# Two transformer blocks on one core: pooling output by token kind, latent-KV columns for context first

## What is computed

```
# pooling layer, for latent tokens and for context tokens
y   = (pooled * silu(gate)) @ w_out            # 2048 x 2048
x   = x   + gate_l * rms_norm(y_lat, post_norm)
ctx = ctx + gate_c * rms_norm(y_ctx, post_norm)
# attention layer
h_lat = rms_norm(x, pre_norm)   * (1 + scale_l) + shift_l
h_ctx = rms_norm(ctx, pre_norm) * (1 + scale_c) + shift_c
proj  = h @ w_in      # 512 cq | 512 ckv | 64 kr | 2048 gate
```

## Time and profile before

| | us |
|---|---|
| median of three runs | 2441.93 (2441.76 to 2445.03) |
| the profiled execution | 2442.31 |
| its span | 2440.5 |
| PE busy in the span | 2247.1 (92%) |
| DVE, ACT busy | 1453.0 (60%), 929.4 (38%) |

### The profile page before, as it was taken

The page is one execution under the profiler, slowest core; times in us unless marked ns, Lnnn a source line. Parts: engine busy times, 40 slices in busy tenths (PEclk is TensorE's granted clock), DMA queues, the critical chain, the costliest instruction groups (busy, mean ns, idle before and its releaser), DMA issues.

```text
span 2440.5 us, 32191 instructions
## 1 busy us (share of the span) xinstructions
PE 2247.1 (92%) x13350; PEld 1819.7 (75%) x13350; DVE 1453.0 (60%) x1894; ACT 929.4 (38%) x1258; POOL 212.1 (9%) x400
## 2 busy tenths in 40 slices
PE   5989899999889999989999999999957999999896
PEld 2678778877878878867777888877836889677575
DVE  1345678777636777746867575676747573334253
ACT  2225445544426545546422222233222333334242
POOL 2211110110010110010000010000010010000000
PEclk8989999999999999999999999999978999999898
DMA  9987576777687676675665464555525585211152
GB/s 373 400 251 275 199 258 216 270 267 258 213 272 264 233 264 230 213 287 188 229 199 181 147 216 139 189 163 178 187 87 176 167 279 148 59 54 56 34 207 103
DMA packets 214858, 496.15 MB, mean 203 GB/s; under 512 B 31616, under 2 KB 35840, under 8 KB 212672
## 3 DMA queue, kind: packets, MB, share of 16 engines
q1 hardware_dynamic: 157728, 278.47, 34.0%
q0 software_dynamic: 56848, 215.38, 25.7%
q10 hardware_dynamic: 144, 0.36, 0.0%
HBM read 485.75 MB, written 8.39 MB: 202 GB/s over the span
## 4 chain that ended last, share of the span: by engine, by line
PE 75%; DVE 9%; DMA 9%; ACT 4%; issue 2%; SPq 1%; POOL 0%; DVEq 0%; ACTq 0%; POOLq 0%
PE ps L733 21%; PE ps L734 20%; PE ps L735 20%; DMA w_raw<-in_w_in 3%; PE ps L788 2%; DMA ada_raw<-in_ada_w 2%; PE ps L1287 1%; PE ps L1285 1%; PE ps L1304 1%; DVE ada_acc L1907 1%; DVE wl L1994 1%; DMA w_raw<-in_w_out 1%; ACT wh L1392 1%; DMA ub<-in_ctx 1%; DMA rsw<-in_ada_w 1%
## 5 line engine op out<-in xcount | busy, mean ns | idle before, releaser
L1994 DVE TENSOR_TENSOR wl<-w_raw,wh 128x1024 fp32r<-128x1024 f32 x280 | 334.8, 1221 | 268.3 <-ACT wh L1392 267.6
L1392 ACT ACTIVATE wh<-w_raw 128x1024 fp32r<-128x1024 f32 x280 | 291.6, 1056 | 439.2 <-PE ps L735 263.9
L733 PE MATMUL ps<-hh,wh 128*128 128x256 f32 x1280 | 375.3, 293 | 11.9 <-DVE hl L2045 7.7
L1987 DVE TENSOR_TENSOR wl<-w_raw,wh 128x1024 fp32r<-128x1024 f32 x194 | 235.1, 1221 | 231.6 <-ACT wh L1445 188.9
L734 PE MATMUL ps<-hh,wl 128*128 128x256 f32 x1280 | 364.0, 284 | 0.0
L735 PE MATMUL ps<-hl,wh 128*128 128x256 f32 x1280 | 363.4, 284 | 0.0
L1907 DVE SCALAR_TENSOR_TENSOR ada_acc<-ada_raw,cpad,ada_acc 128x1024 f32<-128x1024 f32 x272 | 340.7, 1280 | 21.2 <-DMA ada_raw<-in_ada_w 19.0
L1445 ACT ACTIVATE wh<-w_raw 128x1024 fp32r<-128x1024 f32 x162 | 170.1, 1058 | 445.9 <-PE ps L735 407.7
L733 PEld LDWEIGHTS ps<-hh,wh 128*128 128x128 f32 x1280 | 246.0, 192 | 36.2 <-issue 19.7
L733 PE MATMUL ps<-wh,act_hl 128*128 128x512 f32 x640 | 254.9, 398 | 6.7 <-DVE wl L1987 6.7
L734 PE MATMUL ps<-wh,act_hl 128*128 128x512 f32 x640 | 254.3, 397 | 0.0
(11 more groups left out here) (355 smaller groups left out, 3434.7 us busy)
## 6 DMA issues: line engine op xcount, KB each, us to landing
ada_raw<-in_ada_w POOLq DMA_DIRECT2D x272, 512.0 KB, 5.0
w_raw<-in_w_in SPq DMA_DIRECT2D x208, 512.0 KB, 6.5
w_raw<-in_pool_in SPq DMA_DIRECT2D x72, 512.0 KB, 4.6
w_raw<-in_w_out SPq DMA_DIRECT2D x64, 512.0 KB, 5.7
ada_fourth<-in_ada_w POOLq DMA_DIRECT2D x48, 512.0 KB, 6.2
w_raw<-in_mla_in SPq DMA_DIRECT2D x48, 512.0 KB, 4.7
w_raw<-in_pool_out SPq DMA_DIRECT2D x32, 512.0 KB, 4.5
w_raw<-in_mla_out SPq DMA_DIRECT2D x32, 512.0 KB, 3.8
```

The lines of the kernel that those rows point to most:

```text
L733: pe.matmul(dst, ah, bh, start=start, stop=False, skip_group_check=True)
L1392: act.activation(wh[:, g % RING, :], w_raw[:, g % RING, :], ACT.Copy).then_inc(w_hi, 1)
L1987: dve.tensor_tensor(wl[:, r, :], w_raw[:, r, :], wh[:, r, :].bitcast(F32), ALU.subtract).then_inc(w_lo, 1)
L1994: dve.tensor_tensor(wl[:, g % RING, :], w_raw[:, g % RING, :], wh[:, g % RING, :].bitcast(F32), ALU.subtract).then_inc(w_lo, 1)
```

## The change

It cuts the last two quarters of the pooling output into context and latent tokens: stages octx 2, octx 3, olat 2, olat 3 take the place of out 2 and out 3, so the weights of these two quarters are loaded and split twice. It puts ckvc and krc (context columns of ckv and kr) ahead of ckv and kr, which now take latent tokens alone. The residual, norm and transposes of the context tokens are written between slots of olat and those of the latent tokens between slots of ckvc and krc, on all engines. All gate diagonals are made by ACT in out 1. The last two quarters of y are multiplied by the gate row straight from PSUM. x and context are loaded whole by SP. The last four slots of event 21 are summed by PE.

```
-POOL_STAGES += [("out", q, 8, 8) for q in range(4)]
-MLA_STAGES = [("ckv", 0, 8, 8), ("cq", 0, 8, 8), ("kr", 0, 2, 2), ("g", 0, 8, 8), ("g", 1, 8, 6), ("g", 2, 8, 0),
+POOL_STAGES += [("out", 0, 8, (0, 0, 0, 2, 2, 2, 2, 2)), ("out", 1, 8, (2, 2, 2, 0, 2, 2, 1, 1)),
+                ("octx", 2, 8, (0, 0, 0, 0, 1, 0, 1, 0)), ("octx", 3, 8, (1, 0, 1, 0, 1, 0, 1, 0)),
+                ("olat", 2, 8, 0), ("olat", 3, 8, 0)]
+MLA_STAGES = [("ckvc", 0, 8, 0), ("krc", 0, 2, 0), ("ckv", 0, 8, 8), ("cq", 0, 8, 8), ("kr", 0, 2, 2), ("g", 0, 8, 8), ("g", 1, 8, 6), ("g", 2, 8, 0),
...
+                    if kind == "out" and i == 1 and s == 6:
+                        sp.wait_ge(p_grp, 16)
+                        sp.dma_start(xo_c[:, :, :], ctx_in.rearrange("(t p) n -> p t n", p=P)).then_inc(t_x, 16)
+                    if kind == "octx" and i == 3 and s == 4:
+                        sp.wait_ge(stored, 16)
+                        sp.dma_start(xo_l[:, :, :], save_t).then_inc(t_x, 16)
...
-            pool.wait_ge(p_sc, 1)
-            pool.wait_ge(stored, 16)
-            for q in range(4):
-                if q:
-                    pool.wait_ge(t_add, 4 * q)
-                a = slice(q * GRP, (q + 1) * GRP)
-                pool.dma_start(ub[:, 0:TT, :], save_v[:, :, a]).then_inc(t_x, 16)
-                pool.dma_start(ub[:, TT:AT, :], ctx_v[:, :, a]).then_inc(t_x, 16)
+                if i == 6 * ADA_SLOTS + ADA_RING:
+                    pool.wait_ge(t_add, 16)
+                    pool.dma_start(save_v, x4[:, 0:TT, :]).then_inc(stored, 16)
+                ada_load_more(i)
...
@@ PE, pooling output @@
+                        elif s == 2:
+                            pe.wait_ge(p_y, 1)
+                            ada_sums(20, 0)
+                        elif s == 3:
+                            ada_sums_turn(20, 0)
+                        slot_N(g, 4 * i, k0, s == 0, s == n - 1, LAT + CTX_TILES, None if i else 20)
+                    elif kind == "octx":
+                        if i == 2 and s == 4:
+                            pe.wait_ge(t_dg, 1)
+                            pe.wait_ge(p_y, 2)
+                            gate_row(0, 0, 6)
+                            gate_row(0, 1, 7)
+                            gate_row(1, 0, 4)
+                            gate_row(1, 1, 5)
+                        elif i == 2 and s == 7:
+                            pe.wait_ge(t_mul, 2)
+                            gate_row(1, 2, 6)
+                            gate_row(1, 3, 7)
+                        slot_N(g, 2 * (i - 2), k0, s == 0, s == n - 1, CTX_TILES)
+                    else:
+                        if i == 2 and s < ADA_SLOTS - LAST_DVE:
...
+                            ada_slot(ada_buf(m % ADA_RING), LAST_DVE + s, 1, LAST_DVE, None)
+                        elif i == 2 and s == 4:
+                            ada_sums(21, 1, True)
+                        elif i == 2 and s == 5:
+                            ada_sums_turn(21, 1)
+                        elif i == 2:
+                            if s == 6:
+                                gate_row(0, 2, 0)
+                            turn_new_ctx(s - 6)
+                        else:
+                            if s == 2:
+                                pe.wait_ge(p_y, 5)
+                                gate_row(0, 3, 4)
+                            if s < 6:
+                                turn_new_ctx(2 + s)
+                        slot_N(g, 4 + 2 * (i - 2), k0, s == 0, s == n - 1, LAT)
@@ PE, MLA @@
+                    if kind == "ckvc":
+                        for j in {5: (0, 1, 2), 6: (3,), 7: (4,)}.get(s, ()):
+                            turn_new_lat(j)
+                        pe.wait_ge(b_lo, 8 + s + 1)
+                        slot_T(g, 0, k0, s == 0, s == n - 1, SEQ, ctx_=True)
+                    elif kind == "ckv":
+                        pe.wait_ge(h_lo, 8 * DEPTH + 8 + s + 1)
+                        slot_T(g, 0, k0, s == 0, s == n - 1, SEQ)
...
@@ ACT @@
+            def gate_diagonals():
...
+                for v in range(2):
+                    for q in range(4):
+                        for j in range(4):
+                            ins = act.activation(dg2(v, q)[:, j * P:(j + 1) * P], idm, ACT.Copy,
+                                                 scale=mod[:, v, 32 + 4 * q + j:33 + 4 * q + j])
...
+            his_m(0, 4)
+            squares_y(1, 3, 2, 7)
+            his_m(4, 5)
+            rsqrt_std(p_sc, 1, st[:, 14:16], b_std)
+            his_m(5, 6)
+            squares_x(1, 0)
+            his_m(6, 7)
+            squares_x(1, 1)
+            his_m(7, 8)
+            pool_rows_out(21, 1)
+            squares_x(1, 2)
+            his_m(8, 9)
+            squares_x(1, 3)
+            rsqrt_std(b_var, 2, st[:, 10:12], b_std)
...
+            squares_y(0, 3, 6, 11)
+            his_m(20, 21)
+            rsqrt_std(p_sc, 2, st[:, 12:14], b_std)
+            his_m(21, 22)
+            squares_x(0, 0)
+            squares_x(0, 1)
+            his_m(22, 23)
+            squares_x(0, 2)
+            squares_x(0, 3)
+            rsqrt_std(b_var, 3, st[:, 8:10], b_std)
+            his_m(23, 25)
...
@@ DVE @@
+            def gated_y(v, q, y0, row_, rows):
...
+                dve.tensor_copy(x4[:, 2 * v + 1, a], ps[:, row_, :]).then_inc(t_row, 1)
+                dve.wait_ge(t_row, rows - 4)
+                for t in range(TT):
+                    dve.tensor_tensor(x4[:, 2 * v + t, a], ps[:, y0 + t, :], x4[:, 2 * v + 1, a], ALU.mult).then_inc(t_mul, 1)
...
+            def new_x(v, q):
...
+                    dve.scalar_tensor_tensor(x4[:, 2 * v + t, a], x4[:, 2 * v + t, a], st[:, 16 + 2 * v + t:17 + 2 * v + t],
+                                             XO[v][:, t, a], ALU.mult, ALU.add).then_inc(t_add, 1)
...
+            los_m(18, 19)
+            gated_y(0, 3, 6, 4, 8)
+            los_m(19, 20)
+            root(p_y, 6, st[:, 12:14], 24, TT, p_sc)
+            los_m(20, 21)
+            dve.wait_ge(b_std, 4)
+            link(dve.reciprocal(st[:, 16:18], st[:, 12:14]))
+            dve.wait_ge(t_x, 32)
+            new_x(0, 0)
+            new_x(0, 1)
+            los_m(21, 22)
+            new_x(0, 2)
+            new_x(0, 3)
+            los_m(22, 23)
+            root(b_ssq, 12, st[:, 8:10], 48, TT, b_var)
+            dve.wait_ge(b_std, 5)
+            link(dve.reciprocal(st[:, 20:22], st[:, 8:10]))
+            new_diagonals(20, xn_ok)
+            los_m(23, 24)
```

More of the change, by code:

```diff
@@ L190, with ada_more_schedule @@
 ADA_POOL0 = (4 + 6 * DEPTH) * ADA_SLOTS
-ADA_MLA0 = ADA_POOL0 + 6 * ADA_SLOTS
+LAST_DVE = 12
+OLAT0 = MLA0 - 2 * BLK
+KRC0 = MLA0 + BLK
+KR0 = KRC0 + 2 + 2 * BLK
+BEHIND = OLAT0 + 2 * BLK + BLK + 2 + 4
+def ada_more_schedule():
+    slots, dve, after = [], 0, {}
+    for n in range(16, 24):
+        for k in range(ADA_SLOTS):
+            by_pe = n == 21 and k >= LAST_DVE
+            dve += not by_pe
+            slots.append((n, k, by_pe, 6 + k - LAST_DVE if by_pe else dve))
+        after[n] = dve
+    return slots, after
+ADA_MORE, DVE_AFTER = ada_more_schedule()
+PE_SUM = {16: 1, 17: 2, 18: 3, 19: 4, 20: 5, 21: 6 + ADA_SLOTS - LAST_DVE}
+ADA_PE_LAYERS = max(x[5] for x in ADA_SEQ if x[4])
 def both_vectors(n):
@@ L335, in program @@
         phase_p.close()
+        with ExitStack() as phase_o:
+            xo_c = sb("xo_c", [P, TT, D], where=phase_o)
         kvh = sb("kvh", [P, NCH, ALL], F32R)
@@ L344, in program @@
         phase_p.close()
+        with ExitStack() as phase_o:
+            xo_l = sb("xo_l", [P, TT, D], where=phase_o)
         cqh = sb("cqh", [P, NCH, SEQ], F32R)
@@ L2413, in stages, with new_ctx_lo, los_m @@
+            def new_ctx_lo(n):
+                dve.wait_ge(b_hi, 8 + n + 1)
+                dve.tensor_tensor(act_ctx(1, 2 * n, 2), hcm[:, n % 2, :], act_ctx(0, 2 * n, 2).bitcast(F32),
+                                  ALU.subtract).then_inc(b_lo, 1)
+            def los_m(first, last):
+                for g in range(OLAT0 + first, OLAT0 + last):
+                    lo_of(g)
+            def stages(list_, g, after, extras):
                 for kind, i, n, m in list_:
@@ L2425, in stages @@
                             extras("pooled", i)
-                        if s >= mid:
+                        if kind == "out" and i == 1 and s == 6:
+                            pool_ada(20, 0)
+                        if kind == "octx" and i == 2 and s == 7:
+                            first_quarters()
+                        if isinstance(m, tuple):
+                            for _ in range(m[s]):
+                                ada_more()
+                        elif s >= mid:
                             k = -(-left // (n - s))
@@ new lines, in _ @@
+            new_x(1, 3)
+            los_m(7, 8)
+            root(b_ssq, 8, st[:, 10:12], 40, TT, b_var)
+            los_m(8, 9)
+            dve.wait_ge(b_std, 3)
+            link(dve.reciprocal(st[:, 22:24], st[:, 10:12]))
```

(11 more changed lines are left out.)

414 lines of the change are left out of this document (220 added, 194 removed).

## The result

The changed kernel took 2401.47 us (2398.74 to 2408.32 in four runs) where the kernel before took 2443.33 (2441.76 to 2445.03): ratio 0.9833, 95% interval 0.981 to 0.9855. It is 41.9 us faster; the forecast was 36 and a range of 2396 to 2423. The profiled execution is the slowest of the four, 2408.32 us.

The account below looks back on a forecast made before the run. The prediction took a serial chain over DVE, ACT, PE and POOL's loads to bound the bridge, PE elsewhere. 211.0 - 168.9 - 0.7 = 41.4, less 4 and 2, is 35.4, taken as 36: 2442.3 becomes 2406 us, range 2396 to 2423.

Parts of the forecast that it names:

- The bridge: Residual, norm and transposes between last pooling and first MLA product: 74.7 us, PE busy 29.5; a microsecond there shows in the span.
- PE's work, 168.9: PE's work in us from octx to cq in the new kernel, against 211.0 from out 2 to cq before.
- Stalls of 4 us: PE waits in octx 3 (1.5 to 2), olat 2's context transposes (0.5 to 1) and the latent chain (1 to 3).
- Rival 1: In-order queues stall more in octx 3, context chain and latent chain, 3 to 6 us each: 2415 to 2424; chance 0.2.
- Rival 5: Latent chain starts only after olat 3; if its cover fails wholly 17 us come back: 2420; chance counted within Rival 1.
- Loads in ckv and cq, 2 us: In ckv and cq 16.8 MB at 350 GB/s take 48 us against 45.4; less what is buffered, 2 us lost.
- rival 2: Loads bind in ckv and cq at 330 GB/s: 8 to 12 us more, 2414 to 2418; chance 0.1.
- kr's saving becomes wait: After cq, kr needs 5.7 us less of PE, but g 0 waits for low parts behind the kv norm: nothing gained.
- Diagonals cost zero: ACT's 32 gate diagonals in out 1, 6.4 us (12.2 at the upper end), hidden with 6 us spare (2 us).
- SP, POOL and landings: SP's 26 more weight loads fit the ring, 11.2 us per landing (median 4.6); POOL's store of x costs zero.
- rival 3: Slower: narrow slots' loads landing in 11.5 us on average eat the gain; at 12.5, 2454 us; chance 0.06.
- The sum: Gain bound 41.4 us without stalls, minus 4 for stalls and 2 for loads: 35.4, taken as 36.

Follow-up runs that it names:

- ada_early: The changed kernel with seven of event 22's eight layers summed in olat 3 instead of ckv, their loads going out earlier: 2401.18 us, ratio 0.982.
- one_ckv: The changed kernel without ckvc and krc; ckv and kr take both kinds of token, latent chain between olat 3 and ckv: 2416.80 us, ratio 0.9878.
- g0_early: The changed kernel with high and low parts of g 0's first two slots made ahead of the ckv and cq norm: 2406.16 us, ratio 0.9826.
- late: The changed kernel with seven event 22 layers in olat 3, g 0's first parts before the norm, event 23 summed in g 1 and g 2: 2394.29 us.
- no_ada_loads: The changed kernel without layer loads from the fourth of event 22 on, summing old data, last gate wrong: 2400.52 us, ratio 0.9803.
- twice_diagonals: The changed kernel with ACT making the 32 gate diagonals twice over in out 1: 2414.73 us, ratio 0.9872.
- wide_kr: The changed kernel with krc and kr loads in 2 KB rows from other columns, same bytes, kr values wrong: 2404.56 us, ratio 0.9834.

## Why the prediction was right

The verdict, the mechanism and the size were right. Two terms were off, stalls by 3 us too many and loads by 3 to 6 too few, and that they nearly cancel is luck.

- **The bridge is the bound, a microsecond there is one in the span.** Right: 42.1 us gained at the first product of cq, 34.7 to 40.7 from the turn to the end of the span in the three traces, 38.2 to 41.9 by the medians.
- **PE's work, 168.9.** Measured from octx (the product behind the turn of event 20, 1674.86, and five slots of 5.59: 1702.8) to cq 168.4, waits included. The pieces were off both ways. Gate rows took 3.03/4 = 0.76 where I had 0.95, a group of transposes 2.70/3 = 0.90 or less where I had 1.05, a slot of the sum 0.57; the slots made up for it, (36.4 + 22.7 - 6.7)/18 = 2.91 on average in ckvc, krc and ckv against my 2.84, which holds for ckv alone (22.72/8). Octx begins 92.1 us after the turn, 0.6 later than out 2 did (91.5): I had 0.7.
- **Stalls of 4 us, the step that failed.** Octx 3 has none, the diagonals cost 0.7 and 0.3 (1.5 to 2, 0.5 to 1 and 1 to 3 forecast). DVE was busy for 74.9 of 109 us up to the end of olat; ada_early put 9 us more there at no cost. Rival 1, larger handoffs, is out. Rival 5 has a measured price now, a wait of 12.4 us in one_ckv where I had 17 (there without low parts in the chain).
- **Loads in ckv and cq, 2 us, too small.** 5.3 to 7.6. Up to 1.6 us of it is the lower clock behind the waits, which I had at nothing. The mechanism is rival 2's, at 3 to 5.6 us above my term where it said 8 to 12. The two stages took 22.7 + 30.3 = 53.0 us and moved 272 and 290 GB/s; I had used 350, the best stretch of the kernel before. The figure of the Trainium skill (page "DMA: Bandwidth & Descriptors", section "Specifications"), 358 GB/s of HBM for a core, is further off for this mix.
- **kr's saving becomes wait.** Right: 22.50 us from the end of cq to g 0 before, 22.49, 22.49 and 20.80 in the three executions after (the last at a granted clock of 0.91, the two others at 0.87), and in the first the wait at g 0 grew from 1953.81 - 1949.85 = 4.0 to 1923.98 - 1914.50 = 9.5, the 5 us forecast. g0_early shows that an earlier low part does not recover it.
- **Diagonals cost zero.** Right, by 3.9 us. The unit was 0.30, between my bounds (0 and 0.38), above my 0.2.
- **SP, POOL and landings.** Right: weights for octx and olat made ACT wait 1.5 us in all and landed in 5.0, so rival 3 (11.5) was never near. The store's 59.5 us of waiting cost nothing.
- **The sum.** 41.4 - 4 - 2 = 35.4 at the end of cq; measured 34.5, 36.8 and 35.3. By the medians 3 to 7 us more are gained. Where, no trace shows: the traces are single executions, the start of the change alone scatters by 9.3 us, and from the first pair to the end three executions of the changed kernel took 359.7, 359.7 and 364.3 us where the one before took 362.1. In that last part the clock tells them apart, not the work: granted 0.96, 0.96, 0.94 and 0.95, PE busy for 322.1, 322.1, 326.7 and 323.5 us with as many products. I ascribe none of it to the change, and the 3 to 7 us stay open.

Of the signs that I had named for being wrong none appeared: no wait over 10 us, no narrow slot at 3.2 ahead of cq, weights in time in octx. Of the signs for being right one is missing, waits of 4 to 6 us for low parts in octx 3 and ckvc: there are none. The clock is 1.00 up to cq, falls in its last slots and is 0.87 in kr and g 0, where PE still stands (0.85 before).

## What to carry to other kernels

When two chains share a serial bridge, cut the work that feeds it by chain, even if weights are loaded twice: products of one kind then cover the residual and norm of the other, and some 40 of the bridge's 45 idle us came back here. Then look at the stage behind: it meets all the loads that the bridge used to spread out, and a filler job (here sums for a later gate) belongs where both its engine and the queues have room, not where its turn comes. Where a stall is set by the length of an engine's list, reordering the list moves the stall; here it went when the list was made shorter (late), or when the loads that the list waits for were gone (no_ada_loads).

## What I had not expected

The part ahead of the change brings the turn of event 19 at 1605.7 to 1615.0 us in the thirteen executions of the changed kernel and its variants, which are the same up to there: 9.3 us of scatter, as large as most effects sought. From that turn to the last transposes eleven of them, all but one_ckv and twice_diagonals, agree to 0.1 us (236.95 to 237.03). A stage's time counted from a common row settles in one trace what five timed runs leave open, as long as the clock is 1.00. Behind cq it is not enough: from the rope product to the first pair the changed kernel took 91.9 us at clock 1.00 and 93.4 at 0.98, so that a microsecond or two there means little.

At the same DMA share of 0.93 to 0.94 the queues carried from 260 to 326 GB/s in stretches of ten us in ckv and cq. The share says that they are busy, not what they move. The lowest stretch is the one in which kr's narrow rows set out (from 1884.60 us); at the same distance from the turn wide_kr carries 306 GB/s at 0.92, the three unchanged executions 260, 272 and 274 at 0.93 to 0.97, so part of the drop seems to be theirs.
